# Group-norm statistics and normalisation of the mixer output, by heads on ScalarE instead of across heads on VectorE

## The chip, the cores and the metric

The kernel runs on one NeuronCore of a Trainium2 chip. A core has TensorE (PE, the matrix engine, with its weight loads shown as PEld), VectorE (DVE), ScalarE (ACT), GpSimd (POOL), and SyncE (SP), which here only issues DMAs. Each engine works through its own queue in order, and the engines meet through semaphores. The metric is the device time of one execution of the whole program, in microseconds.

## The reference

One decoder layer over a prompt of 1024 tokens and a sample batch of 8 x 8 tokens. The first half of the layer is two token mixers side by side: a retention with 4 heads, and an RWKV-7 recurrence with 8 heads of 64 channels. The part that matters here is what happens to the output `y` of the recurrence, head by head:

```python
y, s_rwkv_new = rwkv7_scan(r4, heads(decay), k4, v4, -kk, kk * a4, s_rwkv.astype(f32))
mean = jnp.mean(y, axis=-1, keepdims=True)
var = jnp.mean((y - mean) ** 2, axis=-1, keepdims=True)
y = ((y - mean) * lax.rsqrt(var + LNX_EPS)).reshape(B, T, RWKV_W) * rwkv_lnx_w + rwkv_lnx_b
bonus = jnp.sum(r4 * k4 * rwkv_r_k, axis=-1, keepdims=True) * v4
y = (y + bonus.reshape(B, T, RWKV_W)) * g
```

So every token has 8 means and 8 variances, each over 64 numbers. After the mixers come an output projection, attention over a memory of 256 tokens, a mixture of 32 experts, and a final norm.

## The kernel before

The program runs in phases, each a block in which every engine has its own instruction list: projection, mixers (span time 333 to 723 us), attention, experts. The next phase starts when all engines have left the block, and its first loads are issued only then.

`phase_mixers` cuts the 1024 prompt tokens into 8 tiles of 128 (partitions are tokens); the sample tokens, 64 rows, are a ninth tile with a shorter code of its own (`NT` is 8, the number of that tile). The prompt tiles are worked in a loop of "pairs": `pair(i)` does the recurrence of tile `i` and, in the gaps, prepares tile `j = i + 1`. The instruction order on each engine is written out by hand in the `pair` function of each engine.

The heart of a pair is a chain that goes round three engines: `level(i, 1)` to `level(i, 5)` build a matrix inverse by doubling. In every level TensorE makes products, VectorE masks them into `X` (line 770), TensorE multiplies again, and ScalarE copies the result from PSUM to `TTT` (lines 1046 and 1044), which the next level needs. In the second level TensorE also waits for `masked`, VectorE's masked products `M4` (line 763). Between level 3 and level 4 TensorE does the product of `rates(j)`. Then come the two steps of the scan (`scan`, copies `sas`, line 1050), and `outputs(i)`; `y_copy(i)` on ScalarE (line 1056) brings `y` to SBUF.

The norm of tile `i` is done one pair later, in `pair(i + 1)`, spread over the chain:

- VectorE `y_center(i)` before its level 2: a reduction to 8 sums (line 785), the mean (line 786), the subtraction (line 787);
- ScalarE `y_square(i)` before its level 3: one Square over 128 x 512 (line 1060);
- VectorE `y_sum(i)` before its level 5: a reduction (line 791) and variance plus epsilon (line 792);
- GpSimd `y_pow(i)`: the power -0.5 on 128 x 8 (line 929), which gives `y_rn`;
- VectorE `y_out(i)` after the first scan step: times the root (line 796), weight, bias, bonus, gate (lines 797 to 803).

For the last prompt tile (number 7) these steps lie among the sample tile's work, and for the sample tile (8) they stand alone at the end of the phase. In the sample tile ScalarE's `SV_sa` copy (line 1128) is what TensorE waits for before it makes the sample's output `y` and then the four groups of products for the new states (`Us`). ScalarE copies `Us` 0 and 2 (line 1134), VectorE 1 and 3 (line 897), and both do so before they turn to the sample's norm.

## Time and profile before

| | us |
|---|---|
| median of 3 runs | 1885.68 |
| lowest, highest | 1878.90, 1887.44 |
| profiled execution | 1887.47 |
| its span | 1885.6 |
| mixers in it | 333 to 723 |
| one pair of it | 38.2 |

The profile is of one execution. The engines' busy times in it add up to far more than the span since they work side by side; what counts is which of them the others wait for in a stretch. TensorE's clock has two levels, 2.4 GHz and 1.2 GHz, shown as a granted clock of 1.0 and 0.5.

### The profile page before, as it was taken

To read this page: it belongs to the slowest core of one execution; us is meant where nothing else is said; L and a number is where in the kernel's file an instruction comes from. 1 tells how busy PE (TensorE), PEld (TensorE's weight loads), DVE (VectorE), ACT (ScalarE), POOL (GpSimd) and SP (SyncE) were. 2 spreads that over 40 slices of the span, in tenths; PEclk is the share of its full clock that TensorE was granted. 3 is DMA by queue.
4 is the path that set the end of the run, shared out by engine and by line. 5 is a ranking of instruction groups with operands and counts; after the bars stand their busy time and mean duration, and the time that the engine had idled before them with its cause. 6 is when DMAs were issued, how large, how long until landed. Compare 5 with 4: busy or idle time off the path is not lost.

```text
span 1885.6 us, 36240 instructions
## 1 busy us (share of the span) xinstructions
PE 1731.7 (92%) x15120; PEld 1438.5 (76%) x15120; DVE 1181.8 (63%) x1365; ACT 830.6 (44%) x962; POOL 297.9 (16%) x269
## 2 busy tenths in 40 slices
PE   7999998889888894899999999878999999999995
PEld 6999887667677773688788888567888888888882
DVE  5544110678888766521434334379999999999995
ACT  5111221444444413500321211137878878878853
POOL 1322000323222220000000000001212212212106
PEclk9999999799999977999999999979999999999997
DMA  7765425311222007744123321969999999999988
GB/s 289 241 195 189 149 67 182 94 56 62 74 73 68 23 2 268 270 173 151 67 67 100 102 79 57 386 248 391 414 416 415 416 409 420 411 415 417 409 328 295
DMA packets 113127, 419.11 MB, mean 222 GB/s; under 512 B 24228, under 2 KB 42728, under 8 KB 84968
## 3 DMA queue, kind: packets, MB, share of 16 engines
q1 hardware_dynamic: 100744, 373.73, 53.2%
q0 software_dynamic: 7072, 25.69, 3.7%
q10 hardware_dynamic: 5184, 17.82, 2.3%
q8 instruction: 102, 1.67, 0.4%
q14 instruction: 25, 0.20, 0.0%
HBM read 350.22 MB, written 75.36 MB: 226 GB/s over the span
## 4 chain that ended last, share of the span: by engine, by line
PE 53%; DVE 3%; DMA 2%; ACT 2%; issue 1%; SPq 0%; POOLq 0%; POOL 0%; DVEq 0%; ACTq 0%
PE banks L2690 27%; PE banks L2220 6%; PE banks L2224 5%; PE banks L2223 5%; PE banks L2216 2%; PE banks L2309 2%; PE banks L2297 1%; PE banks L2565 1%; PE banks L2570 1%; DMA at_ring<-w_out 1%; PE banks L2320 1%; PE banks L2222 1%; DMA ex_raw<-w_e_gate 0%; PE banks L2351 0%; DVE at_x_lo L1736 0%
## 5 line engine op out<-in xcount | busy, mean ns | idle before, releaser
L2813 DVE TENSOR_TENSOR ex_wd_lo<-ex_raw,ex_wd_hi 128x2048 fp32r<-128x2048 f32 x62 | 142.0, 2291 | 36.0 <-ACT ex_wd_hi L2989 36.0
L2813 DVE TENSOR_TENSOR ex_wg_lo<-ex_raw,ex_wg_hi 128x2048 fp32r<-128x2048 f32 x66 | 148.3, 2285 | 4.9 <-ACT ex_wg_hi L2989 2.9
L2813 DVE TENSOR_TENSOR ex_wu_lo<-ex_raw,ex_wu_hi 128x2048 fp32r<-128x2048 f32 x64 | 143.5, 2283 | 0.0
L2989 ACT CAST ex_wd_hi<-ex_raw 128x2048 fp32r<-128x2048 f32 x62 | 118.6, 1914 | 47.6 <-PE banks L2690 29.7
L2989 ACT CAST ex_wu_hi<-ex_raw 128x2048 fp32r<-128x2048 f32 x64 | 122.5, 1915 | 30.0 <-PE banks L2690 30.0
L2989 ACT CAST ex_wg_hi<-ex_raw 128x2048 fp32r<-128x2048 f32 x64 | 122.3, 1912 | 10.0 <-DMA ex_raw<-w_e_gate 3.3
L528 PE MATMUL banks<-pj_w_hi,pj_x_hi 128*128 128x448 f32 (+1 forms) x288 | 109.8, 381 | 11.5 <-DVE pj_x_lo L359 11.5
L528 PE MATMUL banks<-pj_w_lo,pj_x_hi 128*128 128x448 f32 (+1 forms) x288 | 109.5, 380 | 0.0
L2690 PE MATMUL banks<-ex_wg_hi,ex_x_hi 128*128 128x512 f32 x256 | 100.9, 394 | 2.7 <-issue 2.1
L2690 PE MATMUL banks<-ex_wu_hi,ex_x_hi 128*128 128x512 f32 x256 | 102.7, 401 | 0.0
L2690 PE MATMUL banks<-ex_wd_hi,ex_h_hi 128*128 128x512 f32 x248 | 98.1, 396 | 2.8 <-issue 2.8
L2690 PE MATMUL banks<-ex_wg_hi,ex_x_lo 128*128 128x512 f32 x256 | 100.7, 393 | 0.0
L2690 PE MATMUL banks<-ex_wg_lo,ex_x_hi 128*128 128x512 f32 x256 | 100.6, 393 | 0.0
L2690 PE MATMUL banks<-ex_wu_hi,ex_x_lo 128*128 128x512 f32 x256 | 99.9, 390 | 0.0
L2690 PE MATMUL banks<-ex_wu_lo,ex_x_hi 128*128 128x512 f32 x256 | 99.5, 389 | 0.0
L2690 PE MATMUL banks<-ex_wd_lo,ex_h_hi 128*128 128x512 f32 x248 | 98.3, 396 | 0.0
L2650 POOL COPY ex_idx<-moe_slot_tok 128x1 int32 x30 | 35.8, 1194 | 394.1 <-PE banks L2565 388.5
L528 PE MATMUL banks<-pj_w_hi,pj_x_lo 128*128 128x448 f32 (+1 forms) x256 | 97.4, 380 | 0.0
L2690 PE MATMUL banks<-ex_wd_hi,ex_h_lo 128*128 128x512 f32 x248 | 96.9, 391 | 0.0
L1697 POOL TENSOR_TENSOR at_st<-at_st,at_expo 128x1 f32<-128x1 f32 x18 | 9.7, 539 | 482.5 <-DVE at_st L1745 449.8
L528 PE MATMUL banks<-pj_odd_hi,pj_x_hi 128*128 128x448 f32 (+1 forms) x216 | 80.4, 372 | 0.0
L528 PE MATMUL banks<-pj_odd_lo,pj_x_hi 128*128 128x448 f32 (+1 forms) x216 | 80.2, 371 | 0.0
(490 smaller groups left out, 4401.0 us busy)
## 6 DMA issues: line engine op xcount, KB each, us to landing
ex_raw<-w_e_gate SPq DMA_DIRECT2D x64, 1024.0 KB, 8.2
ex_raw<-w_e_up SPq DMA_DIRECT2D x64, 1024.0 KB, 7.3
ex_raw<-w_e_down SPq DMA_DIRECT2D x64, 1024.0 KB, 7.4
blocks<-ex_y ACTq DMA_DIRECT2D x32, 512.0 KB, 7.7
h<-at_h SPq DMA_DIRECT2D x18, 512.0 KB, 2.6
at_slots<-cache_mem_k SPq DMA_DIRECT2D x8, 1024.0 KB, 11.8
at_slots<-cache_mem_v SPq DMA_DIRECT2D x8, 1024.0 KB, 10.8
pj_w<-w_in SPq DMA_DIRECT2D x8, 896.0 KB, 7.1
```

Of the source, the lines that this page charges most:

```text
L528: ins = pe.matmul(PS[:, n % 8, 0:width], xs[:, t, k, :], ws[c % 2][:, k, 0:width], start=k == 0 and a == 0, stop=k == KC - 1 and a == len( ...
L2216: ins = pe.transpose(PS[:, bank + c // 4, c % 4 * P:c % 4 * P + P], src[:, c * P:(c + 1) * P], ident[:])
L2220: pe.matmul(out, hi[:, c, :], w[0][:, c, cols], start=first, stop=False)
L2222: return pe.matmul(out, hi[:, c, :], w[1][:, c, cols], start=False, stop=last)
L2223: pe.matmul(out, hi[:, c, :], w[1][:, c, cols], start=False, stop=False)
L2224: return pe.matmul(out, lo[:, c, :], w[0][:, c, cols], start=False, stop=last)
L2297: ins = pe.matmul(PS[:, 4 + hd // 2, hd % 2 * NMEM:(hd % 2 + 1) * NMEM], qT[:, 2 * hd + c, :], kT[:, 2 * hd + c, :], start=c == 0, stop=c ...
L2309: ins = pe.matmul(PS[:, 6 + cc // 4, cc % 4 * P:cc % 4 * P + P], Vm[:, m, cc * P:(cc + 1) * P], bT[:, cc // 2 * 2 + m, :], start=m == 0, s ...
L2650: po.tensor_copy(idx[:, bf:bf + 1], slot_tok[:, bass.ds(n, 1)]).then_inc(S_("idx"), 1)
L2690: ins = pe.matmul(out, a, b, start=first and i == 0, stop=final and i == 2)
L2813: v.tensor_tensor(w_lo(w), raw[:, j], as_f32(w_hi(w)), ALU.subtract).then_inc(S_("w_split"), 1)
L2989: act.copy(w_hi(home(j, n)), raw[:, j]).then_inc(S_("w_high"), 1)
```

## The change

The sums, the squares and the normalisation of `y` go from whole-tile instructions on VectorE to instructions by head on ScalarE, which can take one bias and one scale per partition and can add up what it writes:

- `y_sums` (ScalarE, new): 8 copies of 128 x 64 with an accumulator give the 8 sums;
- `y_mean` (VectorE, in place of `y_center`): one small instruction gives minus the mean; the subtraction is gone;
- `y_square` (ScalarE): 8 Squares of 128 x 64 with minus the mean as bias and an accumulator, in place of one of 128 x 512;
- `y_sum` (VectorE): the reduction is gone, the small instruction stays;
- `y_shift` (VectorE, new): minus the mean times the root, 128 x 8;
- `y_norm` (ScalarE, new): 8 times `y * root + shift` by head, in place of line 796 on VectorE;
- `y_out` (VectorE) has four instructions in place of five, and waits for `y_norm`.

```diff
@@ vector
-                def y_center(i):
-                    v.wait_ge(S_("y_copied"), i + 1)
-                    lk(v.tensor_reduce(sty[:, 0, :], heads(y[:]), AX.X, ALU.add))
-                    lk(v.tensor_scalar(sty[:, 1, :], sty[:, 0, :], 1.0 / WN, None, ALU.mult))
-                    v.tensor_tensor(heads(y[:]), heads(y[:]), over(sty[:, 1, :], WN), ALU.subtract).then_inc(S_("y_centered"), 1)
+                def y_mean(i):
+                    v.wait_ge(S_("y_summed"), i + 1)
+                    v.tensor_scalar(sty[:, 1, :], sty[:, 0, :], -1.0 / WN, None, ALU.mult).then_inc(S_("y_mean"), 1)
                 def y_sum(i):
                     v.wait_ge(S_("y_squared"), i + 1)
-                    lk(v.tensor_reduce(sty[:, 2, :], heads(yq[:]), AX.X, ALU.add))
                     v.tensor_scalar(sty[:, 3, :], sty[:, 2, :], 1.0 / WN, LNX_EPS, ALU.mult, ALU.add).then_inc(S_("y_sum"), 1)
+                def y_shift(i):
+                    v.wait_ge(S_("y_rn"), i + 1)
+                    v.tensor_tensor(sty[:, 5, :], sty[:, 1, :], sty[:, 4, :], ALU.mult).then_inc(S_("y_shift"), 1)
                 def y_out(i):
-                    v.wait_ge(S_("y_rn"), i + 1)
-                    lk(v.tensor_tensor(heads(y[:]), heads(y[:]), over(sty[:, 4, :], WN), ALU.mult))
+                    v.wait_ge(S_("y_normed"), i + 1)
@@ vector, pair(i)
                     masked(i, 0)
                     masked(i, 1)
+                    level(i, 2)
                     if i >= 1:
-                        y_center(i - 1)
-                    level(i, 2)
+                        y_mean(i - 1)
...
                     ret_out(i)
+                    if i >= 1:
+                        y_shift(i - 1)
                     operands(j)
@@ vector, sample tile
-                y_center(NT - 1)
+                y_mean(NT - 1)
...
                 y_sum(NT - 1)
                 ret_out(NT)
+                y_shift(NT - 1)
                 y_out(NT - 1)
...
-                y_center(NT)
+                y_mean(NT)
                 y_sum(NT)
+                y_shift(NT)
                 y_out(NT)
@@ scalar
+                def y_sums(i):
+                    for h in range(WH):
+                        ins = act.activation(yq[:, hw[h]], y[:, hw[h]], ACT.Copy, accum_out=sty[:, 0, h:h + 1])
+                    ins.then_inc(S_("y_summed"), 1)
                 def y_square(i):
-                    act.wait_ge(S_("y_centered"), i + 1)
-                    act.activation(yq[:], y[:], ACT.Square).then_inc(S_("y_squared"), 1)
+                    act.wait_ge(S_("y_mean"), i + 1)
+                    for h in range(WH):
+                        ins = act.activation(yq[:, hw[h]], y[:, hw[h]], ACT.Square, bias=sty[:, 1, h:h + 1], accum_out=sty[:, 2, h:h + 1])
+                    ins.then_inc(S_("y_squared"), 1)
+                def y_norm(i):
+                    act.wait_ge(S_("y_shift"), i + 1)
+                    for h in range(WH):
+                        ins = act.activation(y[:, hw[h]], y[:, hw[h]], ACT.Identity, bias=sty[:, 5, h:h + 1], scale=sty[:, 4, h:h + 1])
+                    ins.then_inc(S_("y_normed"), 1)
@@ scalar, pair(i)
                     key_square(j)
+                    if i >= 1:
+                        act.wait_ge(S_("y_copied"), i)
+                        y_sums(i - 1)
                     level(i, 1)
...
                     scan(i, 0)
+                    if i >= 1:
+                        y_norm(i - 1)
                     chunk_decays(j)
@@ scalar, sample tile
                 other_half(NT)
+                act.wait_ge(S_("y_copied"), NT)
+                y_sums(NT - 1)
                 y_square(NT - 1)
...
                 level(NT, 2)
+                y_norm(NT - 1)
                 act.wait_ge(S_("sa_s_done"), 1)
                 act.copy(SV[0:NS].rearrange("p q m n -> p (q m n)"), PS[0:NS, 0, :]).then_inc(S_("SV_sa"), 1)
...
+                act.wait_ge(S_("y_copied"), NT + 1)
+                y_sums(NT)
                 y_square(NT)
+                y_norm(NT)
```

Three places show what stands where. First, ScalarE in a pair, from the square of the keys to the copies of level 4; before:

```order
L984 ACTIVATE mx_t0<-mx_kk 128x512
L1046 COPY mx_TTT<-banks 128x512 x2
L1038 COPY mx_x0<-banks 128x512
L1046 COPY mx_TTT<-banks 128x512 x2
L975 COPY mx_qkT<-banks 128x512
L979 COPY mx_loT<-banks 128x128
L980 ACTIVATE mx_hgT<-banks 128x128
L1060 ACTIVATE mx_yq<-mx_y 128x512
L1046 COPY mx_TTT<-banks 128x512 x4
```

and now:

```order
L988 ACTIVATE mx_t0<-mx_kk 128x512
L1064 ACTIVATE mx_yq,mx_sty<-mx_y 128x64 x8
L1050 COPY mx_TTT<-banks 128x512 x2
L1042 COPY mx_x0<-banks 128x512
L1050 COPY mx_TTT<-banks 128x512 x2
L979 COPY mx_qkT<-banks 128x512
L983 COPY mx_loT<-banks 128x128
L984 ACTIVATE mx_hgT<-banks 128x128
L1070 ACTIVATE mx_yq,mx_sty<-mx_y,mx_sty 128x64 x8
L1050 COPY mx_TTT<-banks 128x512 x4
```

Eight activations with an accumulator stand ahead of the level-1 copies of `TTT`, and eight ahead of the level-3 copies in place of one.

Second, ScalarE in the sample tile, from the last `TTT` copies to the end of the phase; before:

```order
L1044 COPY mx_TTT<-banks 128x256 x2
L1128 COPY mx_sas<-banks 64x512
L1131 COPY mx_y<-banks 64x512
L1134 COPY mx_Us<-banks 128x512 x2
L1060 ACTIVATE mx_yq<-mx_y 128x512
L1138 COPY mx_yq<-banks 64x512
```

and now:

```order
L1048 COPY mx_TTT<-banks 128x256 x2
L1076 ACTIVATE mx_y<-mx_y,mx_sty 128x64 x8
L1153 COPY mx_sas<-banks 64x512
L1156 COPY mx_y<-banks 64x512
L1159 COPY mx_Us<-banks 128x512 x2
L1064 ACTIVATE mx_yq,mx_sty<-mx_y 128x64 x8
L1070 ACTIVATE mx_yq,mx_sty<-mx_y,mx_sty 128x64 x8
L1076 ACTIVATE mx_y<-mx_y,mx_sty 128x64 x8
L1166 COPY mx_yq<-banks 64x512
```

The normalisation of tile 7 stands ahead of the copy that writes `SV_sa` (`mx_sas`), and the sample's own norm has three groups of eight.

Third, VectorE in the sample tile, from the eight `spread` instructions (`mx_bx`) on, which it does after its level 2; as it is now:

```order
L881 TENSOR_TENSOR mx_bx<-mx_t1,mx_seq 128x512 x8
L789 TENSOR_SCALAR mx_sty<-mx_sty 128x8
L741 TENSOR_TENSOR mx_rt<-mx_ro,mx_str 64x512
L744 TENSOR_TENSOR mx_o_r<-mx_rt,mx_gr 64x512
L793 TENSOR_TENSOR mx_sty<-mx_sty 128x8
L797 TENSOR_TENSOR mx_y<-mx_y,mx_vec 128x512
```

`y_sum` (line 789), and behind it `y_shift` (line 793), for which the new group on ScalarE waits, stand behind all eight `spread`.

## Rows read from the trace of the kernel before

**Rows 1.** Windows: us; busy PE, PEld, DVE, ACT, POOL (instructions); granted clock, DMA share, GB/s.

```profile
545.49:583.66 38.17, 33.68 (x938) 27.93 (x937) 31.89 (x59) 18.10 (x37) 10.74 (x11) 0.96 0.23 69
554.70:558.11 3.41, 3.34 (x119) 3.03 (x114) 3.14 (x8) 1.17 (x2) 0.00 (x0) 0.51 0.47 129
...
677.58:680.99 3.41, 1.88 (x45) 1.54 (x48) 1.60 (x2) 0.00 (x0) 0.00 (x0) 0.50 0.02 5
```

**Rows 2.** Timeline of ScalarE (start us, duration us, then idle before): the pair 545.49 to 583.66.

```profile
553.15 1.30 ACT L1046 COPY mx_TTT<-banks 128x512 f32<-128x512 f32 x2 [1.03 <-PE banks L1143]
...
559.82 0.64 ACT L1060 ACTIVATE mx_yq<-mx_y 128x512 f32<-128x512 f32 x1
561.09 1.07 ACT L1046 COPY mx_TTT<-banks 128x512 f32<-128x512 f32 x2 [0.63 <-PE banks L1143]
...
576.34 0.27 ACT L1011 ACTIVATE mx_pc<-banks,mx_dbias 128x8 f32<-128x8 f32 x1 [1.89 <-PE banks L1143]
577.31 0.59 ACT L994 COPY mx_gw<-banks 128x512 f32<-128x512 f32 x1 [0.70 <-PE banks L1143]
```

**Rows 3.** Groups of ScalarE by line: count, busy us, mean ns of one.

```profile
L1001 ACT ACTIVATE mx_ex<-banks,mx_dbias 128x512 f32<-128x512 f32 x9 | 6.2, 693 | 3.1 <-PE banks L1143 3.1
...
L1024 ACT ACTIVATE mx_rt<-banks 128x512 f32<-128x512 f32 x8 | 4.8, 600 | 6.9 <-PE banks L1143 6.9
...
L963 ACT ACTIVATE mx_lora<-mx_pin 128x64 f32<-128x64 f32 x6 | 1.6, 259 | 5.0 <-PEq L133 5.0
```

**Rows 4.** Timeline of ScalarE, attention phase: activations with an accumulator.

```profile
1031.46 0.48 ACT L2122 ACTIVATE at_p<-banks,at_st 128x256 f32<-128x256 f32 x1 [15.19 <-DVE at_st L1806]
1031.84 0.20 ACT L2122 ACTIVATION_READ_ACCUMULATOR at_p<-banks,at_st 128x1 f32 x1
1031.93 0.47 ACT L2122 ACTIVATE at_p<-banks,at_st 128x256 f32<-128x256 f32 x1
```

**Rows 5.** Timeline of VectorE, the same pair.

```profile
554.16 0.68 DVE L785 TENSOR_REDUCE mx_sty<-mx_y 128x8 f32<-128x512 f32 x1
...
555.69 0.98 DVE L770 TENSOR_TENSOR mx_X<-banks,mx_lev 128x256 f32<-128x256 f32 x2
...
566.00 0.68 DVE L791 TENSOR_REDUCE mx_sty<-mx_yq 128x8 f32<-128x512 f32 x1
...
566.79 0.75 DVE L770 TENSOR_TENSOR mx_X<-banks,mx_lev 128x256 f32<-128x256 f32 x2
...
574.03 0.69 DVE L721 SCALAR_TENSOR_TENSOR mx_stage<-mx_kk,mx_ex 128x512 f32<-128x512 f32 x1 [0.85 <-ACT mx_ex L1003]
```

**Rows 6.** Timeline of TensorE, the same pair.

```profile
554.39 0.27 PE L1143 MATMUL banks<-mx_TTT,mx_M 64*64 64x64 f32 x2 [0.60 <-DVE mx_M L763]
...
561.42 1.13 PE L1143 MATMUL banks<-mx_wa,mx_loT 64*128 64x512 f32 x4
562.48 1.15 PE L1143 MATMUL banks<-mx_TTT,mx_M 64*64 64x64 f32 x32
```

**Rows 7.** Timeline of ScalarE, the sample tile at the phase's end.

```profile
700.31 0.58 ACT L1128 COPY mx_sas<-banks 64x512 f32<-64x512 f32 x1 [1.48 <-PE banks L1143]
```

**Rows 8.** Timeline of TensorE, same stretch.

```profile
700.94 1.14 PE L1143 MATMUL banks<-mx_sas,mx_M 64*64 64x64 f32 x16 [0.67 <-ACT mx_sas L1128]
...
709.28 1.15 PE L1143 MATMUL banks<-mx_pin,mx_Us 64*64 64x64 f32 x32
```

**Rows 9.** Timeline of GpSimd, same stretch.

```profile
704.58 2.01 POOL L929 TENSOR_TENSOR mx_sty<-mx_sty,mx_expo 128x8 f32<-128x8 f32 x1 [11.20 <-DVE mx_sty L792]
```

**Rows 10.** Timeline of VectorE, same stretch.

```profile
703.61 0.68 DVE L791 TENSOR_REDUCE mx_sty<-mx_yq 128x8 f32<-128x512 f32 x1
...
719.18 0.69 DVE L803 TENSOR_TENSOR mx_o_w<-mx_y,mx_gw 128x512 f32<-128x512 f32 x1
```

**Rows 11.** Timeline of TensorE: one kind of product at full and at half clock.

```profile
546.76 2.91 PE L1143 MATMUL banks<-mx_TQ 64*64 64x64 f32 x128
...
679.72 4.95 PE L1143 MATMUL banks<-mx_TQ 64*64 64x64 f32 x120
```

More of the change, by code:

```diff
@@ L555, in phase_mixers @@
         bonus = sb("bonus", [P, 2, WH])
-        stk, sty, str_ = sb("stk", [P, 3, WH]), sb("sty", [P, 5, WH]), sb("str", [P, 3, RH])
+        stk, sty, str_ = sb("stk", [P, 3, WH]), sb("sty", [P, 6, WH]), sb("str", [P, 3, RH])
         TQ = sb("TQ", [P, 4, HP, P])
```

## The prediction

> **What bounds the kernel now.** The change touches the mixers alone, so I read that phase. First the windows of one pair: in 38.17 us TensorE is busy for 33.68, VectorE for 31.89 and ScalarE for 18.10 [rows 1]. No engine is full and ScalarE has 20 us free, which looks like room for a move. But the pair is a chain round three engines, so what counts is where on ScalarE the free time lies. The timelines tell that. The level-1 copy of `TTT` starts at 553.15 after 1.03 us of idle time, the level-3 copy at 561.09 after 0.63, the copy of `pc` at 576.34 after 1.89 [rows 2]. Those three gaps are where the new groups go. On VectorE, `level` 2 starts at 555.69 and `level` 5 at 566.79 with no idle time noted: there the norm's instructions stand in the way [rows 5]. TensorE begins level 2 at 554.39 when VectorE's `M4` is done, not ScalarE's copy, and level 4 at 562.48, right behind the product of `rates`, which started at 561.42 and took 1.13 [rows 6]. These are the covers the new work can hide behind.
>
> **The price of a small activation.** A 64-wide one without pointers took 259 ns [rows 3]. Every bias or scale that comes from a tile adds something: with a bias 693 ns, without one 600 at the same width, so 93 [rows 3]. With an accumulator there is a second instruction; in the attention phase the read starts 0.10 us before its activation ends, and the next activation 0.09 us after the read's start [rows 4]. So, by head:
> - sum: 0.26 - 0.10 + 0.09 = 0.25, eight are 2.0 us;
> - square (a bias): 0.34, eight are 2.7 us;
> - normalisation (bias and scale, no read): 0.26 + 0.19 - 0.10 = 0.35, eight are 2.7 us (no row has two pointers; I take the step of 93 twice).
>
> Bounds: from the 256-wide activation, whose whole step is 0.47, less 192 columns at 0.85 ns (559.82: 0.64 us for 512 columns, against 0.26 for 64) [rows 2 to 4], a square would be 0.30, eight 2.4. If nothing overlapped, a sum would be 0.26 + 0.20 = 0.46 and a square 0.55, eight 3.7 and 4.4. I take the middle values, since the overlap is in the rows nearest to this pattern; the far end is a rival below.
>
> No row shows an activation with two pointers. The Trainium skill, "ScalarE: Activation LUTs", section "What ACT_TABLE_LOAD costs", gives about 93 ns for each, which agrees with the 93 of the one pointer here; by it the normalisation is an estimated 2.7 us too. The same page's "Rules for kernel authors" sends multiplies and adds to VectorE.
>
> **Sums, ahead of the level-1 copy.** ScalarE's idle time before that copy began at 553.15 - 1.03 = 552.12, so they start at 552.02 [rows 2] and end at 554.0; the first `TTT` copy then ends at 554.6, where TensorE started at 554.39 [rows 6]. That is +0.3 us, since 0.6 us of the delay was TensorE's wait for `M4` anyway. `y_center` is gone from VectorE (the reduction at 554.16 took 0.68, and its other two instructions lay between that and 555.69) [rows 5], but TensorE was busy for 3.34 of the 3.41 us after 554.70 all the same [rows 1], so VectorE did not hold it there: no gain. `y_mean` (0.2 us) stands behind level 2 and before `bonus_sum`, off the chain.
>
> **Squares, ahead of the level-3 copy.** Moved by 0.3 they start at 560.12, take 2.7 and end at 562.82; the copy is done at 563.41. TensorE could start level 4 at 562.48 [rows 6], so level 4 is +0.98 with what came before. Now VectorE: level 4, `rates`, `ret_sum` and `y_sum` run without idle time into level 5. The reduction of `y_sum` (566.00, 0.68 us) is gone, and level 5 starts at 566.79 + 0.98 - 0.68 = 567.09 [rows 5]. So a pair is +0.3 us. With squares of 2.4 us it is 0.0, and if they were hidden wholly behind `rates` -0.4.
>
> **Normalisation, behind the first scan copy.** ScalarE was idle from 574.45 on, for 1.89 us, until `pc` at 576.34 [rows 2]. `y_shift` stands in the 0.85 us of idle time that VectorE has before `operands` at 574.03 [rows 5], and its root was asked for before level 5. The eight run from 574.35 to 577.05, so `pc` comes 0.7 us late. Behind it is the copy of the gate, which waits for TensorE until 577.31 [rows 2], and who needs `pc` (the next retention) needs the gate as well: 0. In `y_out` one instruction less (0.7 us) leads nowhere, since TensorE's next wait is for something earlier. Cover gone (3.6 us instead of 2.7): +0.5.
>
> There are 7 pairs with a norm in them (`i` from 1 to 7): 7 x 0.3 = **+2.1 us** (-3 to +4).
>
> **The sample tile.** Here the order changes more than the load. `y_norm` of tile 7 stands on ScalarE ahead of the `SV_sa` copy, which ran at 700.31 [rows 7]. It waits for `y_shift`, which on VectorE stands behind the eight `spread`, `y_sum` and `ret_out`. The reduction at 703.61 goes [rows 10], so the power starts 0.72 us earlier than 704.58 and ends at 705.87 [rows 9]; `y_shift` takes it to 706.1, eight normalisations to 708.85. The `SV_sa` copy starts at 708.9 instead of 700.31: **+8.6 us** on a wait that did not exist. Behind it in ScalarE's queue are `y_copy` and two `Us` copies. TensorE is what waits: it started the sample's `y` at 700.94 with ScalarE's copy as its releaser, and worked on `y` and the four groups of `Us` products without a break until 709.28 + 1.15 = 710.43 [rows 8]. All that moves by 8.6 to 719.0.
>
> After so long an idle stretch TensorE will restart slow. The same kind of product took 2.91 us for 128 at a granted clock of 1.0 (2.4 GHz) and 4.95 for 120 at 0.5 (1.2 GHz) after little work [rows 1, 11]: 0.55 of the pace. A slow stretch like the 3.41 us of rows 1 loses 1.5 us, twice that 3.1; I take 2.3. [...] So the last product ends at 721.3.
>
> Then the sample's own norm. VectorE copies the last `Us` (0.7) to 722.0, `y_mean` 0.2; meanwhile ScalarE has done its `Us` copies and the sums. Squares 2.7 to 724.9, `y_sum` 0.3, power 2.0 [rows 9], shift 0.2 to 727.4, normalisation 2.7 to 730.1, four instructions of `y_out` at 0.72 to 733.0. The last one ended at 719.18 + 0.69 = 719.87 [rows 10]. **+13.1 us**, and the next phase, whose loads are issued after that, moves as a whole. Bounds: 9.9 with cheap squares, normalisations of 2.1 and 0.8 for the clock; 16 with dear ones and 3.1.
>
> **Sum.** 2.1 + 13.1 = 15.2. Against the profiled execution, 1887.47, that gives 1902.7; it lies 1.8 us above the median of the runs, 1885.68, so for the median I say 1900.9.
>
> **Rivals.**
> - *Not slower than a measurement can tell.* The squares in the pairs cost 2.1 us or less, so that the level-3 copy is ready before the product of `rates` is through (that is the point from which it decides: 8 x 0.26), and VectorE's freed 0.68 us before level 5 reaches the chain. Then -0.4 to -0.7 a pair, -3 to -5 in all, and the tail at its low end: +5 to +7, 1892. For it: VectorE had no idle time at 566.79. Against it: the read after every activation.
> - *Reads don't overlap* at this width. Sums of 3.7 bring level 2 to +2.0, squares of 4.4 level 4 to +4.4, less 0.7: +3.7 a pair, and 0.3 for the normalisation, 28 us in 7 pairs; the tail is +19. Together 47: 1933. Against it: rows 4.
> - *The clock decides.* Every pair has one slow stretch of 3.41 us, at 0.51 [rows 1] in level 2. More waiting in level 3 can bring a second one: 1.5 us each, 7 x 1.5 = +10.5, 1911. Or the shifted work avoids the one there is: 1890.
> - *VectorE was the bound*, and the freed 2.8 us a pair come through by a third: 7 x -0.9 = -6, and the sample's wait is covered by something that I take for ready: 1876 to 1880. The order on ScalarE speaks against it.
>
> **How the numbers follow.** Chances: the forecast 0.60 (its own range +7 to +22; 0.05 of it below 9.4), cheap squares 0.12, no overlap 0.09, a second slow stretch 0.12, the slow stretch avoided 0.05, VectorE the bound 0.02. About 0.5%, 9.4 us, is what a measurement of this kernel can tell from no change: faster 0.02, same 0.05 + 0.12 + 0.05 = 0.22, slower 0.76. The range 1890 to 1915 holds all but the no-overlap case, the faster one and half of the avoided stretch.
>
> **What would show it.** Right: in the trace after, a wait of the `SV_sa` copy's queue for `y_shift` of some 5 us, TensorE idle for 8 us before the sample's `y`, slow clock behind it, and 13 us from there to the phase's end; pairs of 38.2 to 38.8 us; the level-3 copy without idle time before it; level 4's products released by ScalarE instead of following `rates`. Wrong: pairs shorter than 38.0 or longer than 39.5, eight activations with their reads at far from 2.0 and 2.7 us, or an `SV_sa` copy that comes before 705.

## The result, and the profile after

| | before | after |
|---|---|---|
| median, us | 1887.62 (19 runs) | 1902.16 (19 runs) |
| lowest to highest, us | 1874.76 to 1892.54 | 1889.65 to 1907.75 |
| ratio to before | 1 | 1.0077 (95% interval 1.0059 to 1.0096) |
| profiled execution, its span | 1887.47, 1885.6 | 1902.28, 1899.8 |

The change costs 14.5 us, with an interval of 11 to 18. The forecast was 1900.9, 15.2 us above before, and the measured median lies 1.3 us from it. (Before was measured again beside it; the median moved by 2 us.) The lines of the changed file stand up to 28 further down: the copies of `TTT` are now lines 1050 and 1048, the three new groups on ScalarE 1064 (sums), 1070 (squares) and 1076 (normalisation).

From the page after, busy time and share of the span, and the granted clock in 40 slices:

```profile
PE 1737.3 (91%) x15120; PEld 1442.1 (76%) x15120; DVE 1158.5 (61%) x1338; ACT 887.3 (47%) x1313; POOL 296.1 (16%) x269
...
PEclk9999999799889876999999999979999999999997
```

VectorE is 23 us less busy than before (1158.5 against 1181.8), ScalarE 57 us more (887.3 against 830.6). More than two microseconds were added for each one removed.

**The pairs.** The timeline of ScalarE in the pair from 546 to 585 us (start, duration, then what it is), which answers to [rows 2]:

```profile
553.27 0.24 ACT L1064 ACTIVATE mx_yq<-mx_y 128x64 f32<-128x64 f32 x1
553.42 0.19 ACT L1064 ACTIVATION_READ_ACCUMULATOR mx_yq<-mx_y 128x1 f32 x1
553.51 0.24 ACT L1064 ACTIVATE mx_yq<-mx_y 128x64 f32<-128x64 f32 x1
...
555.18 1.04 ACT L1050 COPY mx_TTT<-banks 128x512 f32<-128x512 f32 x2
...
561.69 0.36 ACT L1070 ACTIVATE mx_yq<-mx_y,mx_sty 128x64 f32<-128x64 f32 x1
561.93 0.21 ACT L1070 ACTIVATION_READ_ACCUMULATOR mx_yq<-mx_y,mx_sty 128x1 f32 x1
562.02 0.35 ACT L1070 ACTIVATE mx_yq<-mx_y,mx_sty 128x64 f32<-128x64 f32 x1
...
564.34 1.05 ACT L1050 COPY mx_TTT<-banks 128x512 f32<-128x512 f32 x2
...
576.10 2.77 ACT L1076 ACTIVATE mx_y<-mx_y,mx_sty 128x64 f32<-128x64 f32 x8
578.76 0.27 ACT L1015 ACTIVATE mx_pc<-banks,mx_dbias 128x8 f32<-128x8 f32 x1
579.08 0.59 ACT L998 COPY mx_gw<-banks 128x512 f32<-128x512 f32 x1
```

The gap ahead of the level-1 copies, 1.03 us before, is filled: the copies follow the last accumulator read without idle time. The same holds for the level-3 copies at 564.34, and `pc` and the copy of the gate run back to back behind the normalisation. This pair is not one to take lengths from, since TensorE ran at 1.2 GHz for 6.8 us of it; lengths stand in the table below.

**The sample tile.** ScalarE from the last copies of `TTT` on, which answers to [rows 7]:

```profile
702.19 0.84 ACT L1048 COPY mx_TTT<-banks 128x256 f32<-128x256 f32 x2 [0.93 <-PE banks L1171]
710.29 2.76 ACT L1076 ACTIVATE mx_y<-mx_y,mx_sty 128x64 f32<-128x64 f32 x8 [7.26 <-DVE mx_sty L793]
712.95 0.56 ACT L1153 COPY mx_sas<-banks 64x512 f32<-64x512 f32 x1
716.04 0.58 ACT L1156 COPY mx_y<-banks 64x512 f32<-64x512 f32 x1 [2.52 <-DVE mx_o_w L803]
```

The `SV_sa` copy (now line 1153) starts at 712.95, not 2.3 but 10.8 us after the last `TTT` copies. In front of it stands the normalisation of tile 7, and in front of that 7.26 us in which ScalarE did nothing but wait for `y_shift` (line 793). VectorE in the same stretch, then its last copy of `Us` and the last instruction of the sample's norm ([rows 10] before):

```profile
707.80 0.17 DVE L789 TENSOR_SCALAR mx_sty<-mx_sty 128x8 f32<-128x8 f32 x1
...
710.09 0.17 DVE L793 TENSOR_TENSOR mx_sty<-mx_sty 128x8 f32<-128x8 f32 x1 [0.81 <-POOL mx_sty L933]
713.08 0.69 DVE L797 TENSOR_TENSOR mx_y<-mx_y,mx_vec 128x512 f32<-128x512 f32 x1 [2.83 <-ACT mx_y L1076]
...
725.48 0.69 DVE L900 COPY mx_Us<-banks 128x512 f32<-128x512 f32 x1 [3.48 <-PE banks L1171]
...
736.16 0.69 DVE L803 TENSOR_TENSOR mx_o_w<-mx_y,mx_gw 128x512 f32<-128x512 f32 x1
```

`y_shift` is issued at 710.09, behind `y_sum` (707.80), two instructions of `ret_out`, and GpSimd's power. TensorE ([rows 8] before), and two windows (length; busy PE, PEld, DVE, ACT, POOL; granted clock) over its wait and what follows:

```profile
713.57 1.97 PE L1171 MATMUL banks<-mx_sas,mx_M 64*64 64x64 f32 x16 [9.10 <-ACT mx_sas L1153]
715.46 1.97 PE L1171 MATMUL banks<-mx_bx,mx_sas 128*64 128x512 f32 x4
717.37 1.80 PE L1171 MATMUL banks<-mx_pin,mx_Us 64*64 64x64 f32 x32
719.10 1.08 PE L1171 MATMUL banks<-mx_bx,mx_sas 128*64 128x512 f32 x4
...
724.28 1.15 PE L1171 MATMUL banks<-mx_pin,mx_Us 64*64 64x64 f32 x32
```

```profile
708.00:713.50 5.50, 0.00 (x0) 0.00 (x0) 1.83 (x4) 3.21 (x9) 2.00 (x1) 0.55 0.00 0
713.60:717.00 3.40, 3.40 (x20) 2.04 (x20) 2.25 (x4) 0.58 (x1) 0.00 (x0) 0.50 0.08 27
```

TensorE stands still for 9.10 us with ScalarE's copy as the releaser, and then makes the sample's `y` (713.57) and the first half of the first group of `Us` (715.46) at a granted clock of 0.50: 1.97 us for 16 products that took 1.14 before. The second half of that group (717.37) still takes 1.80 us instead of 1.15; the second group, from 719.10 on, is back at 1.0.

Where the 14.2 us between the two spans come from, by the same events in both traces:

| stretch | before | after | change |
|---|---|---|---|
| `y_copy` of tile 0 to `y_copy` of tile 7 (7 pairs) | 276.66 | 278.67 | +2.0 |
| to the last `TTT` copies of the sample | 31.59 | 33.70 | +2.1 |
| to the start of the `SV_sa` copy | 2.32 | 10.76 | +8.4 |
| to the end of the last `Us` products | 10.12 | 12.48 | +2.4 |
| to the end of the last `y_out` | 9.44 | 11.42 | +2.0 |
| from there to the end of the program | 1165.7 | 1163.0 | -2.7 |

The three lines from the start of the `SV_sa` copy to the last `y_out` (+8.4, +2.4, +2.0, together 12.8) come from the order on ScalarE and what follows it. The first load of the next phase is issued 3.6 us after the last `y_out` before and 3.7 after (723.50 and 740.53), so it moves with it. The first two lines and the last are differences in TensorE's pace that the change does not account for (below).

### The profile page after: what moved, and what is told of

It reads as the page before. It is cut to its first block, busy times and chain, and to the rows that moved or that the text cites. A ratio compares the mean times of both kernels' runs of the same rounds, so it can differ in the third digit from the quotient of the medians.

```text
span 1899.8 us, 36564 instructions
## 1 busy us (share of the span) xinstructions
PE 1737.3 (91%) x15120; PEld 1442.1 (76%) x15120; DVE 1158.5 (61%) x1338; ACT 887.3 (47%) x1313; POOL 296.1 (16%) x269
## 4 chain that ended last, share of the span: by engine, by line
PE 51%; DMA 4%; ACT 2%; DVE 2%; issue 2%; SPq 1%; POOLq 0%; POOL 0%; DVEq 0%; ACTq 0%
PE banks L2718 27%; PE banks L2248 5%; PE banks L2252 5%; PE banks L2251 5%; PE banks L2244 2%; PE banks L2325 2%; PE banks L2337 1%; PE banks L2593 1%; DMA at_slots<-cache_mem_k 1%; DMA at_slots<-cache_mem_v 1%; PE banks L2598 1%; DMA at_ring<-w_out 1%; PE banks L2250 1%; PE banks L2348 1%; DVE at_x_lo L1764 0%
## 5 line engine op out<-in xcount | busy, mean ns | idle before, releaser
L3017 ACT CAST ex_wg_hi<-ex_raw 128x2048 fp32r<-128x2048 f32 x64 | 122.3, 1913 | 10.1 <-DMA ex_raw<-w_e_down 3.7
```

The costliest lines, as they stand in the source:

```text
L3017: act.copy(w_hi(home(j, n)), raw[:, j]).then_inc(S_("w_high"), 1)
```

## The experiments

Theory: the loss is made in the sample tile, by the wait in front of the `SV_sa` copy, the slow clock behind it, and the longer last norm; the pairs cost next to nothing. Rivals: the pairs are the loss, because every activation ahead of a level's copy is on the path; or the clock is.

All ratios are to the kernel before, measured on the same chip, with 95% intervals.

**e1_tail_old.** The new norm in the pairs alone.

```diff
@@ the changed kernel, tiles 7 and 8, all engines
-                y_mean(NT - 1)
+                y_center(NT - 1)
...
-                y_sum(NT); y_shift(NT); y_out(NT)
+                y_sum_old(NT); y_out_old(NT)
...
-                y_sums(NT); y_square(NT); y_norm(NT)
+                y_square_old(NT)
```

> The norm of the prompt tiles 0 to 6 (the seven pairs) as in the changed kernel, that of tiles 7 and 8 as in the kernel before. Theory (the wait ahead of the SV_sa copy and the longer last norm are the loss, the pairs cost little): 2.1 us above before, between -1 and +5, since 7 pairs cost 0.3 us each. Rival (the pairs and the clock's slow stretches in them are the loss): 9 us or more above before, ratio 1.005 or more.

Measured: 1886.60 us, ratio 1.0001 (0.9982 to 1.0019). The pairs cost 0, at most 3.6 us. The expected 2.1 is inside, the rival's 9 us are outside. VectorE in one of its pairs (580.9 to 618.8), level 4 and level 5:

```profile
599.51 0.90 DVE L770 TENSOR_TENSOR mx_X<-banks,mx_lev 128x256 f32<-128x256 f32 x2 [1.62 <-PE banks L1186]
...
602.39 0.42 DVE L770 TENSOR_TENSOR mx_X<-banks,mx_lev 128x256 f32<-128x256 f32 x1
602.98 0.42 DVE L770 TENSOR_TENSOR mx_X<-banks,mx_lev 128x256 f32<-128x256 f32 x1 [0.18 <-PE banks L1186]
```

Counted from the pair's `y_copy`, level 4 starts at 18.61 and level 5 at 21.49 us. In the pair from 583.09 to 621.18 of before they started at 18.21 and 21.79, the latter with no idle time ahead. So the squares put level 4 back by 0.4 us, the missing reduction gives 0.7 back before level 5, and the pair comes out at 37.9 instead of 38.1 us.

One pair is little to go by, since TensorE's slow stretches, those at a granted clock of 0.5, fall in different places in each. Counted from 1, with pair `i` beginning at `y_copy` of tile `i - 1`, pairs 2, 3, 5 and 6 have a single one of 3.4 us in both profiles: they are 37.8, 37.4, 37.9 and 37.9 us long in e1, and 38.0, 38.4, 38.2 and 38.1 in before, in the mean 0.4 less.

**e2_pairs_old.** The reverse: the pairs as before, tiles 7 and 8 new.

```diff
@@ the changed kernel, pair(i), all engines
-                        y_mean(i - 1)
+                        y_center(i - 1)
...
-                        y_sums(i - 1)
...
-                        y_norm(i - 1)
```

> The reverse: the pairs as before, tiles 7 and 8 as in the changed kernel. Theory: 13 us above before (10 to 16), ratio 1.007, with the SV_sa copy some 8 us late and TensorE at half clock behind it. Rival (the pairs are the loss): under 5 us above before.

Measured: 1904.30 us, ratio 1.0098 (1.0069 to 1.0126), 13 to 24 us above before. The whole loss is in the two last tiles. The difference of the medians, 17.7 us, is above the 10 to 16 that were expected; 13 is at the low edge of the interval. In its profile the stretches of the tail are those of the changed kernel (10.8, 12.5 and 11.4 us), so what it has beyond 13 lies elsewhere: 1.4 us ahead of the pairs, 2.0 in the pairs, though these have the old norm, 2.1 before the `TTT` copies and 1.1 behind the mixers. The last `y_out` ends 23.9 us after the `SV_sa` copy starts, as in the changed kernel.

**e3_norm_behind.** One group moved by one place on ScalarE.

```diff
                 level(NT, 2)
-                y_norm(NT - 1)
                 act.wait_ge(S_("sa_s_done"), 1)
                 act.copy(SV[0:NS]...).then_inc(S_("SV_sa"), 1)
+                y_norm(NT - 1)
                 act.wait_ge(S_("y_done"), NT + 1)
```

> The changed kernel with the normalisation of tile 7 behind the SV_sa copy on ScalarE instead of ahead of it, nothing else. Theory (a wait in ScalarE's queue): the SV_sa copy comes right behind TensorE's product, TensorE goes on at full clock, and the end of the phase is bound by the sample's own norm only: 6 us less than the changed kernel, 8 us above before. Rival (the work on ScalarE itself is the cost, wherever it stands): within 2 us of the changed kernel.

Measured: 1893.79 us, ratio 1.0048 (1.0026 to 1.0071), with the same work on every engine. Each taken against its own before, that is 7.3 us less than the changed kernel by the medians and 5.5 by the ratios, whose intervals overlap (1.0026 to 1.0071, 1.0059 to 1.0096). The expected 6 fits; to rule out the rival's 2 us the total alone is weak, and the trace has to decide. ScalarE in its profile:

```profile
698.88 0.58 ACT L1152 COPY mx_sas<-banks 64x512 f32<-64x512 f32 x1 [1.48 <-PE banks L1171]
...
710.41 0.58 ACT L1156 COPY mx_y<-banks 64x512 f32<-64x512 f32 x1 [2.99 <-DVE mx_o_w L803]
```

The `SV_sa` copy has 1.48 us of idle time ahead and TensorE as its releaser, as [rows 7] show of before. It starts 2.32 us after the last `TTT` copies and the last `Us` products end 10.12 us behind it, both as before: the wait (8.4 us) and the slow clock (2.4) are gone. But from there to the last `y_out` pass 15.7 us, where the changed kernel needed 11.4, so the tail is shorter by 6.6 us and not by 10.8. Against before, 6.2 us remain (25.8 from this copy to the last `y_out`, against 19.6): the `y_copy` comes 1.5 us later behind it, since `o_w` of tile 7 is later, and the sample's own norm from `y_copy` on takes 14.3 us instead of 9.6. So the order cost 6.6 us of the tail's 12.8, and the other 6.2 come with the new norm even where it stands in nobody's way.

**e4_filler.** TensorE kept busy in its wait.

```diff
                 ins.then_inc(S_("sa_s_done"), 1)
+                gates = [("spread_dve", h + 1, 4) for h in range(WH)] + [("y_sum", NT, 16), ("y_rn", NT, 4), ("y_shift", NT, 20)]
+                for name, count, times in gates:
+                    pe.wait_ge(S_(name), count)
+                    for n in range(times):
+                        mm(PS[r, 7, n % 8 * 64:(n % 8 + 1) * 64], TTT[r, 0, 0, n % 4, :], TTT[r, 0, 0, n % 4, :])
                 pe.wait_ge(S_("SV_sa"), 1)
```

> The changed kernel with extra products on TensorE, into a bank that nothing reads, while it waits for the SV_sa copy, so that its clock is not slow when the wait ends. Theory (2.4 us of the loss are the slow clock behind the wait): granted clock 1.0 in the 3 us behind the SV_sa copy, the products of y and Us take 9.5 us instead of 11.9, 2 us less in all. Rival (slow for another reason, or the end is bound elsewhere): no difference.

Measured: 1895.99 us, ratio 1.0054 (1.0031 to 1.0077), 5 us under the changed kernel by the medians, each against its own before, and 4 by the ratios, whose intervals overlap. TensorE in its profile:

```profile
710.88 1.14 PE L1171 MATMUL banks<-mx_sas,mx_M 64*64 64x64 f32 x16 [0.29 <-ACT mx_sas L1153]
711.96 1.08 PE L1171 MATMUL banks<-mx_bx,mx_sas 128*64 128x512 f32 x4
...
719.23 1.15 PE L1171 MATMUL banks<-mx_pin,mx_Us 64*64 64x64 f32 x32
```

The 16 products behind the `SV_sa` copy take 1.14 us instead of 1.97, and from the first of them to the end of the last `Us` group pass 9.50 us, against 11.86 in the changed kernel and 9.49 before. That is the 2.4 us. The Trainium skill, "TensorE: Matmul & The Clock Gate", Part 1, says that idleness throttles and activity releases; the granted clock of 0.50 behind the empty wait and of 1.00 behind the filled one agree with it. It does not account for every slow stretch: in the changed kernel TensorE was busy for 13.56 of the 13.65 us from 653.99 to 667.64 by its records and was granted 0.50 all the same. The further 2 to 3 us of this run are not explained by the filled wait; its seven pairs had 30.7 us at 1.2 GHz where the changed kernel's had 44.4, and were 3.2 us shorter.

**e5_sums_only.** The kernel before with the sums alone on ScalarE.

```diff
@@ the kernel before
+                def y_center_summed(i):
+                    v.wait_ge(S_("y_summed"), i + 1)
+                    lk(v.tensor_scalar(sty[:, 1, :], sty[:, 0, :], 1.0 / WN, None, ALU.mult))
+                    v.tensor_tensor(heads(y[:]), heads(y[:]), over(sty[:, 1, :], WN), ALU.subtract).then_inc(S_("y_centered"), 1)
...
                     key_square(j)
+                    if i >= 1:
+                        act.wait_ge(S_("y_copied"), i)
+                        y_sums(i - 1)
```

> The kernel before, but in the seven pairs the 8 sums of y come from ScalarE (8 copies with an accumulator ahead of the level-1 copies); VectorE keeps mean, subtraction, squares' reduction and multiplication. Theory (0.6 us of the sums lie behind TensorE's wait for M4, the rest shows): level 2 of TensorE starts 0.3 us later and a pair is 0 to 0.3 us longer, 0 to 2 us in all, not told from before. Rival (every activation ahead of a level's copy is on the path): 2.0 us a pair, 14 us in all.

Measured: 1892.69 us, ratio 1.0024 (1.0004 to 1.0043), 0.8 to 8 us above before. That is 0.1 to 1.2 us a pair; of the theory's 0 to 2 us only the upper part is inside, and the rival's 14 us are out. The trace tells more. TensorE at the start of level 2, in the pair whose `y_copy` is at 585.72:

```profile
595.36 0.37 PE L1156 MATMUL banks<-mx_TTT,mx_M 64*64 64x64 f32 x2 [0.76 <-ACT mx_TTT L1051]
```

The releaser is now ScalarE's copy and not `M4`, and level 2 starts 9.64 us after `y_copy`, where it started at 9.48 ([rows 6], `y_copy` at 544.91). It is the same in every pair, and in those of e1 and of the changed kernel: +0.16 us. The three pairs with a single slow stretch of 3.4 us in both profiles (2, 3 and 6) are 38.0, 38.1 and 38.3 us long in e5 and 38.0, 38.4 and 38.1 in before. The surplus of e5's profile lies in the others: its seven pairs are 5.8 us longer together and hold 47.8 us at 1.2 GHz instead of 29.8. Whether the sums bring that about no run tells.

**e6_squares_only and e7_squares_late.** The kernel before with the squares by head, at their old place, and behind the level-3 copies.

```diff
@@ the kernel before, scalar
+                def y_squares(i):
+                    act.wait_ge(S_("y_centered"), i + 1)
+                    for h in range(WH):
+                        ins = act.activation(yq[:, hw[h]], y[:, hw[h]], ACT.Square, accum_out=sty[:, 2, h:h + 1])
+                    ins.then_inc(S_("y_squared"), 1)
@@ scalar, pair(i), e6
-                        y_square(i - 1)
+                        y_squares(i - 1)
                     level(i, 3)
@@ scalar, pair(i), e7
-                        y_square(i - 1)
                     level(i, 3)
+                        y_squares(i - 1)
@@ vector, both, in the pairs
-                    lk(v.tensor_reduce(sty[:, 2, :], heads(yq[:]), AX.X, ALU.add))
```

> The kernel before, but in the pairs y is squared by head with an accumulator (no bias, y is centred by VectorE as before), at the same place ahead of the level-3 copies, and VectorE's second reduction is gone. Eight cost 1.9 us in place of 0.64 us. Theory: the level-3 copies are ready just before the product of rates is through, VectorE gives back 0.68 us before level 5, so a pair is 0.3 to 0.6 us shorter, 2 to 4 us less in all. Rival (the squares are on the path whatever their length): 1.2 us a pair more, less 0.7, 3 to 4 us more in all.

> As e6_squares_only, with the squares behind the level-3 copies on ScalarE, where it waited 2.29 us for TensorE before the level-4 copies. Theory: wholly covered there, a pair is 0.5 to 0.7 us shorter than before, 3 to 5 us less in all. Rival (VectorE's reduction was not on the path): the same as before within 1 us.

Measured: e6 1884.78 us, ratio 0.9995 (0.9973 to 1.0017), which does not tell the two expectations apart, though it leaves out most of the rival's 3 to 4 us; e7 1883.68 us, ratio 0.9972 (0.9953 to 0.9992), 1.5 to 9 us less than before. VectorE ahead of level 5 in a pair of e7:

```profile
485.19 0.67 DVE L734 TENSOR_REDUCE mx_str<-mx_rt 128x4 f32<-128x512 f32 x1
485.98 0.17 DVE L796 TENSOR_SCALAR mx_sty<-mx_sty 128x8 f32<-128x8 f32 x1
486.05 0.75 DVE L770 TENSOR_TENSOR mx_X<-banks,mx_lev 128x256 f32<-128x256 f32 x2
```

`ret_sum`, then the small instruction of `y_sum`, then level 5, still without idle time: VectorE's reduction was on the path, and taking it away is worth something. The place of the squares on ScalarE is not told apart by these two runs: pairs 2, 3, 5 and 6, with a single slow stretch each, are 37.4 us long in the mean in e6 and 37.6 in e7, and 38.1 in before. So in the traces the eight squares without a bias are covered at the old place too, and e6's rival (longer pairs) is against them.

**e8_late_and_tail.** e7, and the last two norms earlier in the queues.

```diff
@@ e7_squares_late, vector
                 y_center(NT - 1)
+                y_sum(NT - 1)
                 level(NT, 1)
+                y_out(NT - 1)
                 ret_sum(NT)
...
-                y_sum(NT - 1)
                 ret_out(NT)
-                y_out(NT - 1)
-                for m in (1, 3): ...
                 y_center(NT)
                 y_sum(NT)
+                us_copy(1)
                 y_out(NT)
+                us_copy(3)
@@ gpsimd
+                y_pow(NT - 1)
                 ret_pow(NT)
-                y_pow(NT - 1)
@@ scalar
+                y_square(NT)
                 for m in (0, 2): ...
-                y_square(NT)
```

> e7_squares_late, and in the sample tile the norm of tile 7 stands ahead of the spread instructions on VectorE (in its idle time after level 1), and the norm of the sample ahead of the copies of Us on both engines. Theory (the end of the phase is bound by the norm's place in the queues, not by TensorE's products): the last y_out ends 5 us earlier than in e7, 8 to 10 us less than before in all, ratio 0.995. Rival (bound by the Us products, which end at 710.4, and the stores): 1 to 2 us less than e7.

Measured: 1879.79 us, ratio 0.9953 (0.9934 to 0.9971): faster than before, and some 23 us faster than the changed kernel. VectorE in its sample tile:

```profile
690.99 0.69 DVE L791 TENSOR_REDUCE mx_sty<-mx_yq 128x8 f32<-128x512 f32 x1 [0.70 <-ACT mx_yq L1068]
...
696.63 0.69 DVE L807 TENSOR_TENSOR mx_o_w<-mx_y,mx_gw 128x512 f32<-128x512 f32 x1
...
701.10 4.90 DVE L885 TENSOR_TENSOR mx_bx<-mx_t,mx_seq 128x512 f32<-128x512 f32 x8
...
715.08 0.69 DVE L807 TENSOR_TENSOR mx_o_w<-mx_y,mx_gw 128x512 f32<-128x512 f32 x1
```

Tile 7's norm now ends at 697.3, ahead of the `spread` at 701.10, and the last `y_out` ends 13.0 us after the start of the `SV_sa` copy (702.75), where it was 19.6 before. But the 6.6 us do not reach the next phase. SyncE, which issues the stores and then the next phase's loads:

```profile
710.00 6.77 SPq L653 DMA_DIRECT2D out_rwkv_s<-mx_Us  x4
...
718.49 0.60 SPq L634 DMA_DIRECT2D mixed<-mx_o_w  x1
722.52 0.34 SPq L1621 DMA_DIRECT2D at_h<-mem_prompt  x1
```

The store of `o_w` stands in its queue behind the stores of `Us`, whose last copy VectorE now makes after `y_out`, and is issued 2.7 us after `y_out` is done. From the `SV_sa` copy to the first load of the next phase pass 19.8 us, against 23.2 before (700.31 to 723.50): the tail gave 3.4 us. (A slow stretch lay on the `Us` products of this profile, 11.7 us from the `SV_sa` copy to their end instead of 10.1, so it can give up to 1.5 us more.) By the medians e8 is 3.9 us under e7. The theory is right that the norm's place had bound the end, by 3.4 us; the rival is right that behind it the copies and stores of `Us` do. The intervals of e7 and e8 overlap, so the totals do not tell the theory's 5 us from the rival's 1 to 2.

**e9_squares_twice and e10_norm_twice.** e1 with one group doubled.

```diff
@@ e1_tail_old, scalar, pair(i); e9
+                        for h in range(WH):
+                            act.activation(dup[:, hw[h]], y[:, hw[h]], ACT.Square, bias=sty[:, 1, h:h + 1], accum_out=dups[:, h:h + 1])
                         y_square(i - 1)
@@ e10
+                        for h in range(WH):
+                            act.activation(dup[:, hw[h]], y[:, hw[h]], ACT.Identity, bias=sty[:, 5, h:h + 1], scale=sty[:, 4, h:h + 1])
                         y_norm(i - 1)
```

> e1_tail_old with the group of eight squares run twice in every pair (the first time into a tile that nothing reads), 2.65 us more on ScalarE ahead of the level-3 copies. Theory (the cover behind the product of rates is used up by the first group): all of it shows, 7 x 2.65 = 18 us more than e1_tail_old, ratio to before 1.010. Rival (ScalarE still has room there, as its busy share of one half suggests): under 5 us more.

> e1_tail_old with the group of eight normalisations run twice in every pair (the first time into a tile that nothing reads), 2.65 us more on ScalarE behind the first scan copy. Theory: the first group only just fits, since the copy of the gate came 0.1 us after TensorE's product instead of 0.7 us of idle time; the second shows in full but for 0.1 us at the gate, the retention and the second scan copy wait, 2 to 2.5 us a pair, 14 to 18 us more than e1_tail_old. Rival (the gap there is wide): under 5 us more.

Measured: e9 1911.00 us, ratio 1.0126 (1.0093 to 1.0160); e10 1911.09 us, ratio 1.0140 (1.0102 to 1.0178). Against e1 that is 24 us more by the ratios in e9 and 26 in e10. The added work is 7 x 2.65 = 18.6 us in e9 and 7 x 2.77 = 19.4 in e10. With the intervals of both runs the differences are 16 to 31 and 18 to 34 us, so that more than the added work shows is likely and not certain. Both rivals are out: neither gap has room for a second group. e9 agrees with its 18 us within the interval; e10's 26 us lie above its 14 to 18, with the interval's lower end at 18. The windows of two pairs of e9:

```profile
389.47:432.21 42.74, 35.53 (x937) 29.72 (x938) 29.31 (x56) 27.05 (x91) 10.63 (x11) 0.92 0.21 62
432.21:473.56 41.35, 34.53 (x937) 29.07 (x938) 29.15 (x56) 26.95 (x92) 10.43 (x12) 0.92 0.21 63
```

The granted clock is 0.92 over a pair, where it was 0.96 before ([rows 1]): 6.8 us at 1.2 GHz in each instead of 3.4. Over all seven pairs it is 64.9 us in e9 against 34.1 in e1, and the seven are 302.6 us long against 276.5. So in e9 TensorE waited longer for ScalarE and was also slower when it worked; that the one brings the other is not shown. For e10 the clock explains less: 41.0 us at 1.2 GHz over seven pairs of 299.6 us together. Its two pairs without any slow stretch (2 and 6) were 40.7 and 40.3 us long, where those of e1, with one each, had 37.8 and 37.9. What excess it has stays open.

## Why the prediction was right

**The price of a small activation** held in all three forms. In the rows of after, a sum takes 0.24 us from start to start (553.27 to 553.51; 0.25 was taken), a square 0.33 (0.34), and eight normalisations 2.77 us (2.7; eight steps of the forecast's own 0.35 are 2.8). The single instructions are 240, 343 and 440 ns in the median of 72 each: one pointer adds 103, the second 97. The Trainium skill's 93 ns for each pointer ("ScalarE: Activation LUTs", "What ACT_TABLE_LOAD costs") is near both; no row of before had the second one. The rival in which reads don't overlap is out by the same rows.

**The sums** were to put TensorE's level 2 back by 0.3 us a pair. It is 0.16 in every pair of e1, e5 and after, with ScalarE's copy as the releaser as forecast: right in kind, half the size.

**The squares.** Here the mechanism was right and a size was off. The step was level 4 at +0.98 and level 5 at +0.30. In the pair of e1 shown above level 4 came at +0.4 and level 5 at -0.3. The 0.98 took the square's start, 14.9 us after `y_copy` (559.82), from one pair and added 0.3 for the sums. In the four pairs of before with a single slow stretch the old square began at 14.4 to 14.9, and in the same four of e1 the new ones at 14.3 to 14.7, so not later at all. With that the group ends some 0.6 us sooner than forecast, and less of it sticks out behind the product of `rates`: TensorE starts level 4 at 17.8 in the mean of these four pairs, at 17.5 before. In e1's pair the product of `rates` and the first copy end within 0.1 us of each other, so the sign "released by ScalarE" shows no wait. So a pair costs -0.2 in the one shown and -0.4 in the mean of the four, not +0.3, and seven of them 0 (e1: -3.4 to +3.6) and not 2.1. Why the squares come no later, though level 2 does by 0.16, is not shown; the forecast held that VectorE gives nothing there when `y_center` goes, and no run tests that by itself. The profile of after shows +2.0 over the seven pairs, but it can't be put down to the forecast's reason: TensorE ran at 1.2 GHz for 44.4 us of them, in before for 29.8, and pairs 2, 3 and 6, with a single slow stretch each, are 38.0, 37.8 and 37.4 us long. The forecast had named pairs shorter than 38.0 as a sign of being wrong; two of these are, and it is this term that they mark. That it did not show in the total is partly luck, since it is small against the tail.

**The normalisation behind the scan copy** cost nothing that the runs show: in after the copy of the gate starts at 579.08, right behind `pc`, and e10 shows that the first group has just used up the room, as the 0.7 us said.

**The wait in front of `SV_sa`** was forecast at 8.6 us and is 8.4 (10.76 - 2.32). e3 shows that it is the place in the queue and not the work: one place further back the wait is gone in the trace. (ScalarE's wait for `y_shift` was 7.3 us and not the "some 5" of the signs; the forecast's own times, 706.1 less the end of the `TTT` copies, give 7.3 too.) **The slow clock behind it** was forecast at 2.3 and is 2.4 (12.48 - 10.12, or 11.86 - 9.49 between TensorE's own rows), and e4 took it away. The forecast read its half rate off products that came "after little work"; in before the clock fell at 677.5, and TensorE had been busy for 8.8 of the 10.2 us ahead of that at a granted clock of 1.0. The ratio of the two rates holds, what the engine did before does not. **The last norm** was forecast at 11.7 us from the end of the products, 2.3 more than before; it is 11.42, 2.0 more. Together 12.8 against 13.1. The terms can't be read as what each would give back, though: with the order put right (e3), 6.2 us still remain, where the forecast's split leaves 2.3 to the norm.

**What was not in the sum.** Two differences of about equal size and opposite sign. Before the sample's `TTT` copies 2.1 us were lost, in the products for the retention's state:

```profile
673.06 3.67 PE L1171 MATMUL banks<-mx_bx,mx_qkt 64*64 64x512 f32 x8
678.11 4.08 PE L1171 MATMUL banks<-mx_bx,mx_qkt 64*64 64x512 f32 x8 [1.37 <-DVE mx_Ss L871]
```

These took 2.65 and 2.49 us before, at a granted clock of 1.0. After, the first eight are granted 1.0 too (589 ns each in both); they end 0.6 us later behind `y_copy` since GpSimd's instructions on `mx_bx`, for which they wait, end 0.6 us later. On the second eight a slow stretch lay: 1057 ns each instead of 589. And the phases behind the mixers were 2.7 us shorter, though nothing in them changed (TensorE busy 1079.6 instead of 1085.1 us). The other profiles show that neither belongs to the change. The stretch to the `TTT` copies, 31.6 us in before, is 33.6 to 34.0 in e1, e5, e6, e9 and e10, whose sample tile is worked as in before, and 33.6 to 33.8 in e2, e3 and e4, with the new one; all of these spend 17.1 us of it at 1.2 GHz, before 14.5, and e7, with 10.2, needs 31.0. From the last `y_out` to the end pass between 1161.3 us (e7) and 1168.9 (e9) for the same instructions. It was the profile of before that was fast in the one place and slow in the other. That the two cancel is luck; the range was wide enough for one of them.

Of the clock rival, what is left is scatter, not a direction. Four profiles have the new norm in the pairs and 7 pairs of 278.7, 276.5, 273.4 and 275.5 us (after, e1, e3, e4); two have the old one, 276.7 and 278.7 (before, e2). The same code differs by more than the forecast's 2.1 us. At 1.2 GHz these pairs spent 44.4, 34.1, 27.3 and 30.7 us, and those with the old norm 29.8 and 30.7; the longest seven of the new form are those with the most, but at 29.8 and 30.7 the old form gave 276.7 and 278.7, so the count of slow microseconds alone does not set the length. It weighs, though: from e6 (23.9 slow, 269.9 us) to e5 (47.8 slow, 282.5 us) more of them go with longer pairs. The forecast's premise that every pair has one slow stretch in level 2 was too simple: the first pair of before has none, and its last one, which prepares the sample tile, has 12.8 us of them.

## What to carry to other kernels

When work moves to an engine that looks half idle, ask of each piece what it is queued ahead of and what it waits for itself: here 24 activations a tile were free or nearly so wherever ScalarE already waited, and 10.8 of the tail's 12.8 us arose in and behind one group that waited for VectorE while standing ahead of a copy that TensorE needed. Moving that group back did not return all of it, because a longer chain behind, the sample's own norm, then set the end (e3); after taking a wait away, look for what is bound next. The same holds for e8, where 6.6 us saved on the norm became 3.4 at the next phase. Price an idle stretch of TensorE with the half clock behind it, not only with its own length. And where a pair's timing enters a sum of tenths, take it from several repetitions: in four like pairs of one profile the same square began anywhere from 14.4 to 14.9 us after `y_copy`.

## What the runs showed that I had not expected

Waits in a chain may cost more than their length. Adding 2.65 us of activations to each of seven pairs cost 24 us by the ratios instead of 18.6 (e9), though the intervals do not exclude the 18.6; TensorE spent 64.9 us of these pairs at 1.2 GHz, where the same kernel without the addition spent 34.1. And filling TensorE with useless products (e4) in a wait that exists anyway made the products behind it 2.4 us shorter in the trace, and left the start of the `SV_sa` copy where it was (10.8 us after the `TTT` copies).
